# FoX attention in a two-layer decoder: the pass that multiplies the probabilities by the reciprocal of their sum, on GpSimd instead of VectorE

## What is computed

```
def forgetting_attention(q, k, v, log_f):
    F = jnp.cumsum(log_f, axis=-1)
...
        sc = (jnp.einsum('bhqd,bhkd->bhqk', qi, k) * scale
              + Fi[..., :, None] - F[:, :, None, :])
        sc = jnp.where(k_pos[None, :] <= q_pos[:, None], sc, NEG)
        p = jax.nn.softmax(sc, axis=-1)
        return jnp.einsum('bhqk,bhkd->bhqd', p, v)
```

## Time and profile before

| | |
|---|---|
| median of three runs | 1233.63 us |
| the profiled execution, its own time | 1233.77 us |
| its span | 1232.0 us |
| TensorE busy | 1207.8 us, 98% |
| VectorE, ScalarE, GpSimd busy | 22%, 32%, 43% |
| granted TensorE clock | 0.999 |

### The profile page before, as it was taken

How to read it: one execution, slowest core, us unless ns; L and a number is a source line. 1 busy time by engine, 2 the same in 40 slices (tenths; PEclk the granted TensorE clock), 3 DMA queues, 4 the chain that set the end, 5 groups by cost and what they waited for, 6 DMA issues and landing times.

```text
span 1232.0 us, 14953 instructions
## 1 busy us (share of the span) xinstructions
PE 1207.8 (98%) x5830; PEld 1003.1 (81%) x5830; DVE 272.6 (22%) x467; ACT 390.3 (32%) x585; POOL 528.1 (43%) x287
## 2 busy tenths in 40 slices
PE   7999998999999999999999999999999999999998
PEld 6888886889888888888888888677988888888886
DVE  4720056052111111000051131633411111110003
ACT  5222226334322233212242123743522333222111
POOL 4645531527444444444437435024644444445430
PEclk9999999999999999999999999999999999999999
DMA  7444202224322222322223234012322222322311
GB/s 279 130 128 137 103 1 91 81 70 137 103 101 86 102 101 87 103 99 89 86 97 126 98 104 158 18 36 68 121 96 92 102 96 92 102 94 94 103 52 69
DMA packets 33465, 120.96 MB, mean 98 GB/s; under 512 B 3683, under 2 KB 3939, under 8 KB 33164
## 3 DMA queue, kind: packets, MB, share of 16 engines
q1 hardware_dynamic: 30328, 109.94, 25.9%
q10 hardware_dynamic: 3092, 10.37, 2.9%
HBM read 116.87 MB, written 3.42 MB: 98 GB/s over the span
## 4 chain that ended last, share of the span: by engine, by line
PE 90%; DVE 4%; POOL 2%; ACT 2%; DMA 1%; issue 1%; DVEq 0%; POOLq 0%; SPq 0%; ACTq 0%
PE ps L836 28%; PE ps L837 28%; PE ps L838 28%; PE ps L992 2%; PE ps L958 2%; POOL w_lo L237 1%; DVE work L608 1%; DVE x L611 1%; DMA w_raw<-weights 1%; PE ps L978 1%; PE ps L1054 1%; PE ps L1045 1%; DVE work L623 1%; ACT squares L378 1%; PE ps L865 1%
## 5 line engine op out<-in xcount | busy, mean ns | idle before, releaser
L237 POOL TENSOR_TENSOR w_lo<-w_raw,w_hi 128x1024 fp32r<-128x1024 f32 x200 | 479.8, 2416 | 571.9 <-ACT w_hi L340 571.7
L836 PE MATMUL ps<-h_hi,w_hi 128*128 128x512 f32 (+1 forms) x1088 | 396.9, 365 | 2.9 <-DVE h_lo L629 2.9
L837 PE MATMUL ps<-h_lo,w_hi 128*128 128x512 f32 (+1 forms) x1088 | 396.1, 364 | 0.0
L838 PE MATMUL ps<-h_hi,w_lo 128*128 128x512 f32 (+1 forms) x1088 | 396.1, 364 | 0.0
L340 ACT ACTIVATE w_hi<-w_raw 128x1024 fp32r<-128x1024 f32 x201 | 210.5, 1057 | 357.0 <-DMA w_raw<-weights 349.4
L836 PEld LDWEIGHTS ps<-h_hi,w_hi 128*128 128x128 f32 x1088 | 205.2, 189 | 37.2 <-DVE h_lo L629 4.8
L837 PEld LDWEIGHTS ps<-h_lo,w_hi 128*128 128x128 f32 x1088 | 205.3, 189 | 32.4
L838 PEld LDWEIGHTS ps<-h_hi,w_lo 128*128 128x128 f32 x1088 | 205.3, 189 | 32.2
L836 PE MATMUL ps<-w_hi,prod_hi 128*128 128x512 f32 x352 | 137.1, 390 | 0.0
L838 PE MATMUL ps<-w_hi,prod_lo 128*128 128x512 f32 x352 | 136.9, 389 | 0.0
L837 PE MATMUL ps<-w_lo,prod_hi 128*128 128x512 f32 x352 | 136.9, 389 | 0.0
(11 more groups left out here) (107 smaller groups left out, 740.4 us busy)
## 6 DMA issues: line engine op xcount, KB each, us to landing
w_raw<-weights SPq DMA_DIRECT2D x201, 512.0 KB, 3.2
x<-x_in SPq DMA_DIRECT2D x4, 512.0 KB, 7.2
gain_pre<-norms ACTq DMA_DIRECT2D x4, 512.0 KB, 4.6
gain_post<-norms ACTq DMA_DIRECT2D x4, 512.0 KB, 4.6
minus_f<-forget_rows ACTq DMA_DIRECT2D x1, 2048.0 KB, 10.9
out<-x SPq DMA_DIRECT2D x3, 512.0 KB, 2.6
bias_rows<-bias_row ACTq DMA_DIRECT2D x1, 1280.0 KB
decay<-decay_in ACTq DMA_DIRECT2D x1, 1024.0 KB
```

The costliest lines, as they stand in the source:

```text
L237: nc.gpsimd.tensor_tensor(w_lo[:, c % RING], w_raw[:, c % RING], w_hi[:, c % RING].bitcast(F32), ALU.subtract).then_inc(lo_done, 1)
L836: mm(to, held[0], moved[0], start=start, stop=False)
L837: mm(to, held[0], moved[1], start=False, stop=False)
L838: return mm(to, held[1], moved[0], start=False, stop=stop)
```

## The change

Line numbers after the change are some 1 to 13 higher than before. In the FoX attention VectorE keeps the reciprocal and drops the pass over `work`. The reciprocal signals a new semaphore `inverted`. GpSimd has a new function `scale_probs`, which waits for `inverted` unit by unit and does the pass, and it is that pass which signals `probs` to TensorE. GpSimd's queue is cut at chunk OUT1+6 to let these 32 passes in, and the 14 low parts ahead of the cut and the 6 behind it are written out one by one, where a loop took the first 16 of these 20. In the MoBA attention VectorE still does both, and waits for its own reciprocal on `inverted` in place of `vec_step`.

```diff
+        inverted = sem("inverted")
...
+            def scale_probs(heads, unit0):
+                for m in range(TILES * heads):
+                    u, i = unit0 + m, QUERY_ORDER[m % TILES]
+                    row = work[:, m % 4, 0:(i + 1) * P]
+                    pool.wait_ge(inverted, u + 1)
+                    nc.gpsimd.tensor_scalar(row, row, row_rec[:, u:u + 1], None, ALU.mult).then_inc(probs, 1)
+
...
-                    at = GATE1 + 1
+                    lows(GATE1 + 1, OUT1 + 6)
+                    scale_probs(FOX, TILES * MOBA)
+                    at = OUT1 + 6
...
-                        own(nc.vector.reciprocal(row_rec[:, u:u + 1], row_sum[:, u:u + 1]))
-                        nc.vector.tensor_scalar(work[:, m % 4, 0:(i + 1) * P], work[:, m % 4, 0:(i + 1) * P],
-                                                row_rec[:, u:u + 1], None, ALU.mult).then_inc(probs, 1)
+                        nc.vector.reciprocal(row_rec[:, u:u + 1], row_sum[:, u:u + 1]).then_inc(inverted, 1)
+                        if heads == MOBA:
+                            vec.wait_ge(inverted, u + 1)
+                        if heads == MOBA:
+                            nc.vector.tensor_scalar(work[:, m % 4, 0:(i + 1) * P], work[:, m % 4, 0:(i + 1) * P],
+                                                    row_rec[:, u:u + 1], None, ALU.mult).then_inc(probs, 1)
```

## The result

The changed kernel takes 1237.28 us (median of 8 runs, 1237.06 to 1237.47); the kernel before takes 1233.59 us beside it. The ratio is 1.003, with a 95% interval of 1.0021 to 1.004. So the change costs 3.7 us, where I had forecast 0.1, and the time lies 0.8 us beyond the upper end of my range. The profiled execution took 1237.17 us.

What follows compares the result with a forecast made beforehand. TensorE, busy 98% of the span, was taken as the bound. All terms were 0 but unit 4's +0.10 us: 1233.77 to 1233.87, with the median 0.14 lower, so forecast 1233.7 us, range 1233.2 to 1236.5.

Steps and rivals of the forecast that it cites:

- What bounds the stage, and where the pass has the least room: FoX attention: TensorE's order bounds it; the narrowest place in a head is its first, widest unit (512 columns).
- kind-0 loads: TensorE's loads of the transposed blocks of each head's first, 512-column unit; six steady ones were predicted to cost 0.
- unit 4: A 512-column unit while the pipeline still fills; 0.64 us left for the pass, predicted cost 0.10 us.
- The room, 0.92 us: Time left for GpSimd's pass between reciprocal and TensorE's load at six steady 512-column units: 1.28 us less reciprocal and hand overs.
- X = 0.196 + 512 x 1.07 ns = 0.74 us: Estimated time of the 512-column pass on GpSimd, from half the two-input slope; bounds 0.49 and 1.287 us.
- The sum: Formula 6 x (X - 0.92) + (X - 0.64), each term only above zero; +0.10 us in all, X being the 512-column pass time.
- the first rival: GpSimd's 512-column pass is as slow as two-input operations, 1.287 us: cost 2.85 us, 1236.5 us; chance 0.20 above 1.23.
- point of decision, 1.23 us: Time of GpSimd's 512-column pass above which the cost passes 2.5 us and the forecast counts as wrong.
- The lock: Rival: VectorE and GpSimd lock each other out of SBUF in the FoX stage; 1234.3 us, chance 0.05.
- VectorE's relief: Taking 12.38 us of pass off VectorE in FoX: forecast gain 0; as rival at most 1.7 us, 1232.0 us, chance 0.03.
- the two waits: TensorE's waits before the loads of units 3 (0.87 us) and 29 (0.81 us), claimed to end with ScalarE's copies.
- The range: Whole kernel: 1233.2 to 1236.5 us, from a free 512-column pass on GpSimd to the 2.85 us cost of two-input pace.

## Why the prediction was wrong

- *What bounds the stage, and where the pass has the least room.* Right. TensorE's order bounds it; the loss is at the kind-0 loads and at unit 4, as the runs with a part of the passes and with the early reciprocal show.
- *The room, 0.92 us.* Nearly right. The hand over from GpSimd to TensorE, which I took from ScalarE's 0.12, is 0.05 (793.61 + 1.57 = 795.18 to 795.23), so the room is 0.99, and 0.71 at unit 4.
- *"X = 0.196 + 512 x 1.07 ns = 0.74 us."* This is the step that failed. It measured 1.564 us. I reasoned that a second input that isn't read can't cost, halved the slope of the two-input form, and called that form's row a bound from above: "an operation with one input fewer has no reason to take longer". What the runs show in its place is that the form sets the price: TENSOR_SCALAR takes 2.50 ns per column where two wide inputs take 2.13 and a copy 0.83. I had named the scalar operand as the risk, and it is only 0.07 us. The only TENSOR_SCALAR rows that I had the earlier trace rows were one and four columns wide and tell nothing of a slope. The Trainium skill's "1-input is roughly line-rate" (GPSIMD Engine Reference, Engine selection) fits the copy and not this form.
- *The sum.* With X = 1.564 my formula gives 6 x 0.644 + 0.924 = 4.79 us, 0.49 less by the shorter hand over at seven places, and 0.57 less by what the end gives back, which I had left out: 3.73, against 3.76 in the rows. The mechanism was that of the first rival, whose price of 2.85 us was too low by the same wrong bound. Its point of decision, 1.23 us, was passed.
- *The lock.* VectorE's L694 isn't drawn out beside GpSimd's pass: 0.56 us for 384 columns while the pass of unit 16 ran (second line below), the same 0.56 as in the kernel before, where GpSimd is idle there (first line). The Trainium skill's rule (SBUF — State Buffer, Who interferes with whom), that VectorE with at most one SBUF input and outside its two-port modes doesn't contend, agrees with it. And the four widths of the pass lie on one line, whatever VectorE did beside them.

```profile
792.58 0.56 DVE L684 CUSTOM_DVE_ANT_0 work<-ps,minus_f 128x384 f32<-128x384 f32 x1
...
794.18 0.56 DVE L694 CUSTOM_DVE_ANT_0 work<-ps,minus_f 128x384 f32<-128x384 f32 x1 [0.66 <-PE ps L974]
```

- *VectorE's relief.* Right: 0, shown by leaving the pass out. That ScalarE's copies end the two waits was right too. Incomplete was that ScalarE's order there "hangs on scores": at unit 29 it was the exponent of unit 30, placed ahead of the copy, and exchanging the two took 0.65 us off the wait.
- *The range.* It ended at 1236.5 since it took the two-input row for the end of X. A form that no wide row shows needed an end beyond its neighbours.

## What to carry to other kernels

Before a pass is moved to an engine that sits idle, read how long TensorE (or whoever bounds the stage) can wait for it at the narrowest unit, from the last thing that the pass needs to the load that uses it; a full engine-time balance (here the four passes of a head take 4.3 us of 5.7) tells nothing of that. A price from another form of instruction is an estimate and not a bound, however alike the two look: on GpSimd the form alone moved the price per column by a factor of three. Where the slow engine must do the pass, first look for what stands ahead of it without need, as the reciprocal here stood behind the next unit's logits. And where a load of TensorE waits for several engines, compare the ends of all of them with its start: the name in the bracket was VectorE's at both waits of the kernel before, and ScalarE's copy ended them.

## What was unexpected of the hardware

GpSimd's price per column depends on the form more than on what is read: copy 0.83 ns, TENSOR_TENSOR with a repeated input 1.66, with two wide inputs 2.13, TENSOR_SCALAR 2.50 with a constant as with a scalar from SBUF (float32, 128 partitions). Multiplying by a scalar is so a third faster on this engine if it is written as a product of two tensors. TensorE's load starts 0.05 us after the end of GpSimd's pass, and 0.12 us after the end of ScalarE's copy.
